# Four changes of order on TensorE in a fused decoder block: residual transposes, score pairs, probability transposes, first square sum

## The chip, the cores and the metric

The kernel runs on one core of a Trainium2 chip. The metric is the device time of one execution in microseconds (us); the times given are of three runs, and one more execution was recorded by the hardware profiler. Engines are called as the profile calls them: PE is TensorE (matmuls), PEld its weight loads, DVE is VectorE, ACT is ScalarE, POOL is GpSimd, SP is SyncE, which here issues the DMAs.

## What is computed

One decoder block on 256 tokens of width 1024, in float32: a hybrid mixer (a convolution branch and a dilated attention branch with 12 heads of 64, both gated), then a retrieval layer that picks 16 of 16384 single-neuron experts for each of 8 heads. Cut to what matters:

```python
xn = rmsnorm(x, norm1_g)
proj = xn @ w_in                                  # GLU input, q, k, v, gates
conv_out = conformer_conv(glu_in, ...)            # 31 taps, layernorm, silu, projection
q, k = rmsnorm(q, q_norm_g), rmsnorm(k, k_norm_g) # per head
s = q @ k.T * scale + bias[head, distance]        # per head, causal, dilated windows
p = exp(s - logsumexp(s)) ; o = p @ v             # times a weight per head group
merged = sigmoid(g_conv) * conv_out + sigmoid(g_attn) * (o @ attn_w_proj)
x = x + merged @ mix_w_out
hn = rmsnorm(x, norm2_g)
q = hn @ w_q ; s = q . sub_keys ; top 16 of 16 x 16 candidates ; gate = softmax
h = u_tab[e] . hn ; act = gelu(h) * gate ; y = x + sum(act * v_tab[e])
```

## The kernel before

**Tiles.** All weights come as tiles of 128 x 1024 float32 (512 KB), through a ring of four slots. Tiles 0 to 75 are the front: 0 to 7 GLU, 8 to 19 q and k, 20 to 25 v, 26 to 41 gates, 42 to 47 attention projection, 48 to 51 convolution projection, 52 to 59 mixer output, 60 to 75 the queries of the retrieval (`wq` 0 to 15, "query tiles"). Then 128 tiles of `u_tab` and 128 of `v_tab` follow in loops. Each tile is split into a high part (ACT, `split_hi`, L335) and a low part (POOL or DVE, `split_lo`, L354); the activations are split as well, so one tile is 8 blocks times 3 products (high by high, high by low, low by high): 24 matmuls at L1218, L1319 or, for the first tiles, L1242 and L1249. A tile's slot is loaded again when its low part is there, ACT and POOL work three tiles ahead of PE.

**Order.** `jobs_in_order()` (L81) writes out by hand, tile by tile, which results PE makes in the front; the tables `SCORES_AT`, `TURN_AT`, `ATTEND_AT` and others say after which tile small jobs stand. From this list come the number of PE's step that each consumer waits for, and the PSUM bank of each job (`BANK_OF`, L130): six banks in turn up to the first transposed probabilities, then seven, then eight, and from the first mixer tile on banks 4 to 7 only. `start(job)` lets PE wait until the bank's previous job has been read by ACT or DVE. For the third query tile and those behind it this is the query tile or square sum four jobs ahead, so `wq` 3 waits for DVE's scaled copy of `wq` 0 (L982).

**The places of the change.**
- `first_tiles()` (L1253): the first three GLU tiles are multiplied before the norm of x is known; behind them stands the sum of squares `ssq1` (L1265, `ones` by `sq`). ACT takes its root (L493), DVE its reciprocal (L764), and all of DVE's and ACT's later work on the norm, up to the high and low parts of the normed x that tile 8 needs, hangs on it. In DVE's queue the last addition of squares (L760) stands behind the low part of tile 3 (`lo_of(3)`).
- `scores(two)` (L1325): two score jobs at a time. Job s is for token half c = s // 6 and the pair of heads `PAIRS[s % 6]`, which are (0, 2), (1, 3), (4, 6), (5, 7), (8, 10), (9, 11). An even head lies in SBUF partitions 0 to 63 of its q and k block, an odd one in 64 to 127, and so in rows 0 to 63 or 64 to 127 of the array. For c = 0 a head's product has 128 columns, for c = 1 it has 256. The loop alternates between the two jobs: first head of one, first head of the other, second heads.
- On DVE `score(s)` (L818, L825) adds the bias and takes the maximum, on ACT `exp_of(s)` takes the exponentials (L507), both counting on semaphores in order.
- `turn(h)` (L1340) transposes a head's probabilities, three blocks of 128 x 128; `attend(bl)` (L1349) multiplies two heads' transposed probabilities with the values. The four slots of `pT` are used in turn, so the copy of head h's transposes waits for the product that read head h - 4.
- The residual transposes (L1440): 16 transposes of the new residual x into banks 0 to 3, where the retrieval's result is then accumulated. POOL fills `iota_nk` (L456) after them, on the semaphore `y_began`.
- `q_sums`, `k_sums`, `spread_k`: norms of q and k. `spread_k` (L1306) needs `rk_parts` from DVE (L900), which stands in DVE's queue between the taps of the depthwise convolution (L794, L798).

Of the kernel before, what the change touches and what calls it, by code (L numbers as in the profile page):

```python
# [15 lines left out]
P = 128  # L16
D = 1024
T = 256
KB = D // P
TC = T // P  # L20
# [43 lines left out]
QSS_AT, KSS_AT, KB_AT = 16, 20, 22  # L64
SCORES_AT = {24: (0, 1), 25: (2, 3), 26: (4, 5), 27: (6, 7), 28: (8, 9), 30: (10, 11)}
WEIGHTS_AT = 32
# [16 lines left out]
def jobs_in_order():  # L83

    order = []
    for n in range(T_ATT):
        if n < T_QK:
            order.append((("glu", n), n))
            if n == 2:
                order.append((("ssq1",), None))  # L90
        elif n < T_V:
            order.append((("qk", n - T_QK), n))
        elif n < T_GATE:
            order.append((("v", (n - T_V) // 2) if (n - T_V) % 2 else None, n))
        else:
            order.append((("gate", n - T_GATE), n))
        order += [(("bias", h), None) for h in BIAS_AT.get(n, ())]
        if n == QSS_AT:
            order.append((("qss",), None))
        if n == KSS_AT:  # L100
            order.append((("kss",), None))
        if KB_AT <= n < KB_AT + AB // 2:
            order.append((("kb", n - KB_AT), None))
        order += [(("score", i), None) for i in SCORES_AT.get(n, ())]
        if n == LNSUM_AT:
            order.append((("lnsum",), None))
        if n == LNVAR_AT:
            order.append((("lnvar",), None))
        order += [(("o", bl), None) for bl in ATTEND_AT.get(n, ())]
        order += [(("pT", h), None) for h in TURN_AT.get(n, ())]  # L110
    for b in range(KB):
# [54 lines left out]
def hybrid_block(nc, x_t, front, cols, rel_bias, onehot, sub_keys, u_tiles, v_tiles, out):  # L166
    bias_row = nc.dram_tensor("bias_row", (HEADS, BW), F32, kind="Internal").ap()
    toeplitz = nc.dram_tensor("toeplitz", (HEADS, P * BW), F32, kind="Internal").ap()
    with ExitStack() as ctx:
# [295 lines left out]
        def _(a):  # L465
# [34 lines left out]
            def exp_of(s):  # L500
                c, pair = divmod(s, len(PAIRS))
                w = P * (c + 1)
                a.wait_ge(score_max, s + 1)
                for h in PAIRS[pair]:
# [197 lines left out]
        def _(dve):  # L702
# [50 lines left out]
            for i in range(2):  # L753
# [3 lines left out]
                   .then_inc(pair_sums, 1)  # L757
            lo_of(3)
            dve.wait_ge(pair_sums, 2)
            dve.tensor_tensor(sq[:, 0:2, :], sq[:, 0:2, :], part_, ALU.add).then_inc(pair_sums, 1)  # L760
            dve.wait_ge(prm_in, 16)
            dve.tensor_tensor(gains[:, :], prm[:, C_QG:C_QG + 1], prm[:, C_KG:C_KG + 1], ALU.mult).then_inc(gains_ready, 1)
# [47 lines left out]
            def score(s):  # L810
# [12 lines left out]
                freed(dve, ("score", s))  # L823
                dve.wait_ge(biased, s + 1)
                dve.tensor_reduce(negm[:, c * HEADS + h0:c * HEADS + h0 + 3:2], p3[:, h0:h0 + 3:2, c * P:c * P + w],  # L825
# [39 lines left out]
            def attention_after(n):  # L865
                for b in ATTEND_AT.get(n, ()):
                    low_o(b)
                for h in TURN_AT.get(n, ()):
                    if freed_by_dve(("pT", h)):
                        copy_pT(dve, dve.tensor_copy, h)  # L870

            for n in range(T_ATT):
# [325 lines left out]
        def _(pe):  # L1198
# [54 lines left out]
            def first_tiles():  # L1253

                b0, b1, b2 = [start(("glu", n)) for n in range(3)]
                high_products(b0, 0)
                high_products(b1, 1)
                low_products(b0, 0)
                low_products(b1, 1)
                high_products(b2, 2)  # L1260
                low_products(b2, 2)
                b = start(("ssq1",))
                pe.wait_ge(pair_sums, 3)
                for k in range(2):
                    ins = pe.matmul(b[:, 0:T], ones[:, :], sq[:, k, :], start=k == 0, stop=k == 1)  # L1265
                step(ins)

            def two_tiles(jobs, tiles, parts_ready, vec_hi, vec_lo):
# [56 lines left out]
            def scores(two):  # L1325

                c = two[0] // len(PAIRS)
                w = P * (c + 1)
                banks = [start(("score", s)) for s in two]
                freed(pe, ("kb", two[0] % len(PAIRS) // 2))  # L1330
                for r in range(2):
                    for b, s in zip(banks, two):
                        h = PAIRS[s % len(PAIRS)][r]
                        rows = slice((h % 2) * HD, (h % 2 + 1) * HD)
# [27 lines left out]
            for n in range(T_ATT):  # L1362
# [38 lines left out]
                if n == min(TURN_AT):  # L1401
                    pe.wait_ge(tap, CB * TAPS)
                    freed(pe, ("v", AB // 2 - 1))
                for bl in ATTEND_AT.get(n, ()):
                    attend(bl)
                for h in TURN_AT.get(n, ()):
                    turn(h)
            for b_ in range(KB):
# [24 lines left out]
            for u in range(2, HALVES):  # L1433
                step(full(T_WQ + u, ("wq", u), xg_hi, xg_lo))
                if u == 2:

                    freed(pe, ("mix", KB - 1))
                    for c in range(TC):
                        for k in range(KB):
                            ins = pe.matmul(bank[2 * c + k // 4][:, (k % 4) * P:(k % 4 + 1) * P],  # L1440
                                            resid[:, k, c * P:(c + 1) * P], ident[:, :], is_transpose=True,
                                            start=k % 4 == 0, stop=False, skip_group_check=True)
                    ins.then_inc(y_began, 1)
            assert done[0] == FRONT_STEPS
            pe.wait_ge(sk_in, 16)
            for j in range(N_SC):
# [181 lines left out]
```

## Time and profile before

| | |
|---|---|
| median of 3 runs | 996.57 us (996.49 to 997.5) |
| the profiled execution | 997.07 us, span in the profile 995.2 us |
| PE busy | 989.8 us, 99% of the span |
| DVE, ACT, POOL busy | 774.9, 506.8, 465.3 us |
| granted clock of PE | 1.0 of full speed |
| front (tiles 0 to 75 and the scores of the keys) | to about 259.5 us |
| u tiles, v tiles | 259.5 to 626, 626 to 992 us |

An ended line of the timeline gives start, duration, engine, source line, operation and operands; rows of one kind that follow each other are merged ("x8"), and a matmul's duration holds its latency, so the pace of PE is read from starts, or from the chain of waits, whose rows run from one start of a group to about the next. A float32 matmul is two records, an fp32r matmul and a transpose one.

### The profile page before, as it was taken

Reading aid. Unit: us, or ns where it says so; the run is one execution under the profiler, and the core shown is the slowest. Engines: PE = TensorE matmul, PEld = TensorE weight load, DVE = VectorE, ACT = ScalarE, POOL = GpSimd, SP = SyncE. Lnnn points to the kernel's source line nnn. Section 1 sums busy time; section 2 is a strip of 40 time slices with the busy share of each in tenths; the row PEclk is TensorE's granted clock in tenths of the full one; section 3 lists DMA queues with packets and bytes.
Section 4 is the critical chain, followed back from the end, with each engine's and each line's share of the span. In section 5 each row is a group of like instructions: output and inputs, shape, how many; then the busy total and the mean of one; then the engine's idle time right before and its main releaser. Section 6 shows DMA issues by size and latency. Waiting matters only on the chain.

```text
span 995.2 us, 21854 instructions
## 1 busy us (share of the span) xinstructions
PE 989.8 (99%) x7822; PEld 917.0 (92%) x7822; DVE 774.9 (78%) x1304; ACT 506.8 (51%) x789; POOL 465.3 (47%) x198
## 2 busy tenths in 40 slices
PE   9999999999999999999999999999999999999998
PEld 9998999999999999999999999888888888888887
DVE  5999784868899996097777777988888876776764
ACT  6663877544555544544444444444444445554443
POOL 3664366656689999874444444100000004344442
PEclk9999999999999999999999999999999999999999
DMA  6684445654455565555555555555554555556562
GB/s 242 211 308 150 149 148 162 212 201 149 150 197 200 171 211 188 191 176 184 177 180 174 182 172 169 185 175 170 177 180 171 182 174 190 190 189 195 186 203 90
DMA packets 52619, 181.95 MB, mean 183 GB/s; under 512 B 5943, under 2 KB 9155, under 8 KB 52452
## 3 DMA queue, kind: packets, MB, share of 16 engines
q1 hardware_dynamic: 52292, 181.16, 54.4%
q8 instruction: 25, 0.41, 0.2%
q10 hardware_dynamic: 288, 0.27, 0.1%
q14 instruction: 14, 0.11, 0.0%
HBM read 180.33 MB, written 3.43 MB: 185 GB/s over the span
## 4 chain that ended last, share of the span: by engine, by line
PE 93%; DVE 5%; ACT 1%; issue 0%; POOL 0%; ACTq 0%; DVEq 0%; POOLq 0%
PE bank L1218 50%; PE bank L1527 35%; DVE bank L798 3%; PE bank L1476 3%; PE bank L1319 1%; PE bank L1233 1%; PE bank L1451 1%; DVE lo L354 1%; PE bank L1242 1%; PE bank L1553 1%; PE bank L1335 1%; ACT hi L335 0%; PE bank L1358 0%; PE bank L1346 0%; PE bank L1249 0%
## 5 line engine op out<-in xcount | busy, mean ns | idle before, releaser
L354 POOL TENSOR_TENSOR lo<-raw,hi 128x1024 fp32r<-128x1024 f32 x184 | 462.4, 2527 | 515.9 <-ACT hi L335 515.4
L335 ACT CAST hi<-raw 128x1024 fp32r<-128x1024 f32 x332 | 348.0, 1049 | 218.0 <-PE bank L1527 186.3
L1218 PE MATMUL bank<-norm_space,hi 128*128 128x256 f32 x2624 | 452.4, 278 | 0.2 <-POOL lo L354 0.2
L1218 PEld LDWEIGHTS bank<-norm_space,hi 128*128 128x128 f32 x2624 | 396.2, 188 | 1.8 <-issue 1.2
L1218 PE MATMUL bank<-norm_space,lo 128*128 128x256 f32 x1312 | 362.8, 277 | 0.0
L1527 PE MATMUL bank<-hi,norm_space 128*128 128x512 f32 x1008 | 273.8, 391 | 0.0
L1218 PEld LDWEIGHTS bank<-norm_space,lo 128*128 128x128 f32 x1312 | 246.4, 188 | 0.0
L1527 PEld LDWEIGHTS bank<-hi,norm_space 128*128 128x128 f32 x1008 | 188.0, 188 | 38.5
L354 DVE TENSOR_TENSOR lo<-raw,hi 128x1024 fp32r<-128x1024 f32 x148 | 189.2, 1279 | 27.4 <-ACT hi L335 27.3
L1527 PE MATMUL bank<-lo,norm_space 128*128 128x512 f32 x504 | 155.5, 390 | 0.0
L1145 DVE TENSOR_TENSOR norm_space<-act,norm_space 128x256 fp32r<-128x256 f32 x128 | 111.7, 876 | 48.8 <-ACT norm_space L665 48.8
L645 ACT ACTIVATE act<-bank 128x256 f32 (+1 forms) x128 | 49.2, 384 | 187.8 <-PE bank L1218 187.8
L1527 PEld LDWEIGHTS bank<-lo,norm_space 128*128 128x128 f32 x504 | 94.6, 188 | 19.7
L1218 PE MATMUL bank<-rounded_space,hi 128*128 128x256 f32 x496 | 87.0, 280 | 0.0
L1138 DVE SCALAR_TENSOR_TENSOR act<-bank,act 128x512 f32 (+1 forms) x64 | 41.4, 686 | 51.7 <-PE bank L1476 51.7
L1126 DVE TENSOR_TENSOR ohB<-eqB,parts 128x1024 f16<-128x1024 f16 x64 | 81.4, 1272 | 0.0
L1218 PEld LDWEIGHTS bank<-rounded_space,hi 128*128 128x128 f32 x496 | 75.4, 188 | 0.9 <-issue 0.6
L1218 PE MATMUL bank<-rounded_space,lo 128*128 128x256 f32 x248 | 69.1, 278 | 0.0
L665 ACT CAST norm_space<-act 128x256 fp32r (+1 forms) x128 | 51.4, 402 | 0.1
L1218 PEld LDWEIGHTS bank<-rounded_space,lo 128*128 128x128 f32 x248 | 47.0, 190 | 0.0
L798 DVE SCALAR_TENSOR_TENSOR bank<-u_pad,prm,bank 128x256 f32<-128x256 f32 x116 | 46.3, 481 | 0.0
L1122 DVE TENSOR_TENSOR ohA<-iota_nk,keys 128x1024 f16<-128x1024 f16 x64 | 46.1, 720 | 0.0
(183 smaller groups left out, 651.5 us busy)
## 6 DMA issues: line engine op xcount, KB each, us to landing
raw<-u_tiles SPq DMA_DIRECT2D x128, 512.0 KB, 3.3
raw<-v_tiles SPq DMA_DIRECT2D x128, 512.0 KB, 3.3
raw<-front SPq DMA_DIRECT2D x76, 512.0 KB, 3.8
toeplitz<-bias_row SPq DMA_DIRECT2D x6, 384.0 KB, 7.5
bias<-toeplitz SPq DMA_DIRECT2D x12, 128.0 KB, 3.5
resid<-x_t SPq DMA_DIRECT2D x2, 512.0 KB, 4.7
qk<-sub_keys SPq DMA_DIRECT2D x1, 1024.0 KB, 8.0
y<-act SPq DMA_DIRECT2D x3, 256.0 KB, 2.0
```

Source lines behind the costliest of these rows:

```text
L335: act_e.copy(hi[:, s, :], raw[:, s, :]).then_inc(hi_ready, 1)
L354: eng.tensor_tensor(lo[:, s, :], raw[:, s, :], hi[:, s, :].bitcast(F32), ALU.subtract)\
L645: a.activation(act[:, it * 4 + (base_i + j), :], bank[4 + j % 2][:, 0:T], ACT.Gelu).then_inc(gelu_done, 1)
L665: a.copy(act_hi[:, (base_i + j) % RING, :], act[:, it * 4 + (base_i + j), :]).then_inc(a_hi, 1)
L798: dve.scalar_tensor_tensor(out=acc[:, b, :] if w == TAPS - 1 else part_sum, in0=src, scalar=wt, in1=part_sum, op0=ALU.mult, op1=ALU.add).t ...
L1122: dve.tensor_tensor(ohA[:, g % 2], every_pair(iota_nk[:, :, :], NK), at(keys[:, 0, t], NK), ALU.is_equal).then_inc(spread, 1)
L1126: dve.tensor_tensor(ohB[:, g % 2].rearrange("p a i n b -> p (a i) n b"), eqB[:, :, :, :].unsqueeze(2).broadcast_to([P, TOK // PAIR, 2, HAL ...
L1138: dve.scalar_tensor_tensor(out=av, in0=gv, scalar=1.0 / GATE_SCALE, in1=av, op0=ALU.mult, op1=ALU.mult)\
L1145: dve.tensor_tensor(act_lo[:, s, :], act[:, it * 4 + (base_i + j), :], act_hi[:, s, :].bitcast(F32), ALU.subtract).then_inc(a_lo, 1)
L1218: ins = pe.matmul(dst, w_[:, s, u * P:(u + 1) * P], x_[:, k, :], start=first and i == 0 and p_ == 0, stop=last and i == n - 1 and p_ == 2)
L1476: ins = pe.matmul(bank[6 + g][:, q * HALF:(q + 1) * HALF], ohA[:, g, q // PAIR, :, q % PAIR], ohB[:, g, q // PAIR, i, :, q % PAIR], start= ...
L1527: ins = pe.matmul(bank[2 * c + half][:, :], a_[:, j, c * P:(c + 1) * P], v_[:, j, half * 512:(half + 1) * 512], start=False, stop=False, s ...
```

## The change

Four edits, and what follows from them in the counters:

1. The residual transposes go from behind `wq` 2 to behind `wq` 15, ahead of the key scores (L1451).
2. `SCORES_AT` pairs a job of the second token half with the job of the first half for the same heads: (6, 0), (7, 1) and so on, where it was (0, 1), (2, 3). `SCORE_PLACE` gives each job's place in the new order for the two semaphores that count.
3. Behind tiles 38 and 39 the transposes of the probabilities (`pT`) come ahead of the products with the values (`o`), on PE, in the bank order and on DVE. ACT's order stays.
4. `ssq1` comes behind the second tile, the third tile behind it; DVE's last addition of squares comes ahead of the low part of tile 3.

```diff
-SCORES_AT = {24: (0, 1), 25: (2, 3), 26: (4, 5), 27: (6, 7), 28: (8, 9), 30: (10, 11)}
+SCORES_AT = {24: (6, 0), 25: (7, 1), 26: (8, 2), 27: (9, 3), 28: (10, 4), 30: (11, 5)}
+SCORE_PLACE = {s: i for i, s in enumerate(s for n in sorted(SCORES_AT) for s in SCORES_AT[n])}
...
-            if n == 2:
+            if n == 1:
                 order.append((("ssq1",), None))
...
+        order += [(("pT", h), None) for h in TURN_AT.get(n, ())]
         order += [(("o", bl), None) for bl in ATTEND_AT.get(n, ())]
-        order += [(("pT", h), None) for h in TURN_AT.get(n, ())]
...
-                a.wait_ge(score_max, s + 1)
+                a.wait_ge(score_max, SCORE_PLACE[s] + 1)
...
-            lo_of(3)
             dve.wait_ge(pair_sums, 2)
             dve.tensor_tensor(sq[:, 0:2, :], sq[:, 0:2, :], part_, ALU.add).then_inc(pair_sums, 1)
+            lo_of(3)
...
-                c = two[0] // len(PAIRS)
-                w = P * (c + 1)
                 banks = [start(("score", s)) for s in two]
                 freed(pe, ("kb", two[0] % len(PAIRS) // 2))
                 for r in range(2):
                     for b, s in zip(banks, two):
-                        h = PAIRS[s % len(PAIRS)][r]
+                        c, pair = divmod(s, len(PAIRS))
+                        w = P * (c + 1)
+                        h = PAIRS[pair][r]
...
             for u in range(2, HALVES):
                 step(full(T_WQ + u, ("wq", u), xg_hi, xg_lo))
-                if u == 2:
-
-                    freed(pe, ("mix", KB - 1))
-                    for c in range(TC):
...
+            freed(pe, ("mix", KB - 1))
+            for c in range(TC):
+                for k in range(KB):
+                    ins = pe.matmul(bank[2 * c + k // 4][:, (k % 4) * P:(k % 4 + 1) * P],
+                                    resid[:, k, c * P:(c + 1) * P], ident[:, :], is_transpose=True,
+                                    start=k % 4 == 0, stop=False, skip_group_check=True)
+            ins.then_inc(y_began, 1)
```

On PE at its first products (L1242 and L1249 are high and low part of a tile, bank0 and bank1 the first two tiles), before:

```order
L1249 MATMUL bank1<-rounded_space,lo 128x256 x8
L1242 MATMUL bank2<-rounded_space,hi 128x256 x16
L1249 MATMUL bank2<-rounded_space,lo 128x256 x8
L1265 MATMUL bank3<-sq,ones 128x256 x2
L1218 MATMUL bank4<-rounded_space,hi 128x256 x2
```

and after (lines are numbered one or two higher):

```order
L1250 MATMUL bank1<-rounded_space,lo 128x256 x8
L1264 MATMUL bank2<-sq,ones 128x256 x2
L1243 MATMUL bank3<-rounded_space,hi 128x256 x16
L1250 MATMUL bank3<-rounded_space,lo 128x256 x8
L1219 MATMUL bank4<-rounded_space,hi 128x256 x2
```

The square sum now stands ahead of the third tile's 24 products.

On PE the first call of `scores`, behind tile 24, before (bank1 is score job 0, heads 0 and 2; bank2 is job 1, heads 1 and 3):

```order
L1335 MATMUL bank1<-qk 128x128
L1335 MATMUL bank2<-qk 128x128
L1335 MATMUL bank1<-qk 128x128
L1335 MATMUL bank2<-qk 128x128
```

and after (bank1 is job 6, heads 0 and 2 for the second token half; bank2 is job 0, heads 0 and 2 for the first):

```order
L1337 MATMUL bank1<-qk 128x256
L1337 MATMUL bank2<-qk 128x128
L1337 MATMUL bank1<-qk 128x256
L1337 MATMUL bank2<-qk 128x128
```

Each of the six calls now has one wide and one narrow job, and all four of its matmuls are of heads of the same parity.

On PE at the end of the front, after the change, behind the last query tile:

```order
L1441 MATMUL bank0<-ident,resid 128x128 x4
L1441 MATMUL bank1<-ident,resid 128x128 x4
L1441 MATMUL bank2<-ident,resid 128x128 x4
L1441 MATMUL bank3<-ident,resid 128x128 x4
L1451 MATMUL bank7<-qk,prob 128x128 x4
L1451 MATMUL bank4<-qk,prob 128x128 x4
```

The sixteen transposes stood between `wq` 2 and `wq` 3, whose products now follow each other directly.

## Rows read from the trace of the kernel before

**Rows 1.** The page: busy time, share of the span and instructions of each engine.

```profile
PE 989.8 (99%) x7822; PEld 917.0 (92%) x7822; DVE 774.9 (78%) x1304; ACT 506.8 (51%) x789; POOL 465.3 (47%) x198
```

**Rows 2.** Waits of PE: who is waited for, us in total, times, longest.

```profile
PE bank L1306 <- DVE rk_parts L900: 0.8, 1, 0.8
PE bank L1218 <- POOL lo L354: 0.2, 1, 0.2
```

**Rows 3.** Chain that ended last: start us, us, what. Two score calls, key scores.

```profile
91.27 0.65 PE bank L1335 x8
...
102.10 1.06 PE bank L1335 x8
...
252.52 7.14 PE bank L1451 x64
```

**Rows 4.** Timeline: start us, us, engine, line. Weight loads beside the square sum's matmuls.

```profile
210.24 0.59 PE L1431 MATMUL bank<-sq,ones 128*128 128x256 f32 x2
210.46 0.40 PEld L1432 LDWEIGHTS bank<-sq,ones 128*128 128x128 f32 x2
210.67 0.59 PE L1432 MATMUL bank<-sq,ones 128*128 128x256 f32 x2
```

**Rows 5.** Chain that ended last, long stretches of tiles at two paces.

```profile
153.06 57.34 PE bank L1218 x504
...
215.77 36.75 PE bank L1218 x312
```

**Rows 6.** Timeline of PE and DVE around the residual transposes.

```profile
212.46 1.75 DVE L989 RECIPROCAL rs<-rs 128x256 f32<-128x256 f32 x1 [3.36 <-ACT rs L633]
214.25 0.42 DVE L982 TENSOR_TENSOR prob<-bank,rs 128x256 f32<-128x256 f32 x1
```

```profile
213.86 1.91 PE L1440 MATMUL bank<-ident,resid 128*128 128x128 f32 x16
215.52 0.48 PE L1218 MATMUL bank<-rounded_space,hi 128*128 128x256 f32 x2
```

**Rows 7.** Timeline of DVE, from the squares to the first tap.

```profile
13.20 0.69 DVE L756 TENSOR_TENSOR bank<-sq,bank 128x512 f32<-128x512 f32 x1
...
19.48 1.75 DVE L764 RECIPROCAL rs<-rs 128x256 f32<-128x256 f32 x1 [2.96 <-ACT rs L493]
...
28.16 1.22 DVE L354 TENSOR_TENSOR lo<-raw,hi 128x1024 fp32r<-128x1024 f32 x1
...
35.34 0.43 DVE L777 TENSOR_TENSOR bank<-bank,rs 128x256 f32<-128x256 f32 x1 [0.24 <-PE bank L1218]
...
38.67 2.78 DVE L354 TENSOR_TENSOR lo<-raw,hi 128x1024 fp32r<-128x1024 f32 x1 [0.57 <-ACT hi L335]
41.38 1.88 DVE L794 TENSOR_SCALAR bank<-u_pad,prm 128x256 f32<-128x256 f32 x4
```

**Rows 8.** Timeline of ACT: high parts of tile 4, root, tiles 5 and 6.

```profile
16.29 1.05 ACT L335 CAST hi<-raw 128x1024 fp32r<-128x1024 f32 x1 [2.22 <-DMA raw<-front]
19.06 0.38 ACT L493 ACTIVATE rs<-bank 128x256 f32<-128x256 f32 x1 [1.72 <-PE bank L1265]
...
20.76 2.00 ACT L335 CAST hi<-raw 128x1024 fp32r<-128x1024 f32 x2
```

**Rows 9.** Timeline of POOL: low parts of tiles 5 and 6, then 8 to 10.

```profile
21.89 4.77 POOL L354 TENSOR_TENSOR lo<-raw,hi 128x1024 fp32r<-128x1024 f32 x2 [2.09 <-ACT hi L335]
32.92 7.44 POOL L354 TENSOR_TENSOR lo<-raw,hi 128x1024 fp32r<-128x1024 f32 x3 [6.27 <-ACT hi L335]
```

**Rows 10.** Timeline of PE: two tile starts, at 24.44 and 35.47.

```profile
24.22 0.28 PE L1218 MATMUL bank<-rounded_space,lo 128*128 128x256 f32 x1
24.44 0.47 PE L1218 MATMUL bank<-rounded_space,hi 128*128 128x256 f32 x2
...
35.02 0.28 PE L1218 MATMUL bank<-rounded_space,lo 128*128 128x256 f32 x1
35.47 0.47 PE L1218 MATMUL bank<-norm_space,hi 128*128 128x256 f32 x2 [0.17 <-POOL lo L354]
```

More of the change, by code:

```diff
@@ L823, in score @@
                 freed(dve, ("score", s))
-                dve.wait_ge(biased, s + 1)
+                dve.wait_ge(biased, SCORE_PLACE[s] + 1)
                 dve.tensor_reduce(negm[:, c * HEADS + h0:c * HEADS + h0 + 3:2], p3[:, h0:h0 + 3:2, c * P:c * P + w],
@@ L865, in attention_after @@
             def attention_after(n):
-                for b in ATTEND_AT.get(n, ()):
-                    low_o(b)
                 for h in TURN_AT.get(n, ()):
@@ L870, in attention_after @@
                         copy_pT(dve, dve.tensor_copy, h)
+                for b in ATTEND_AT.get(n, ()):
+                    low_o(b)
             for n in range(T_ATT):
@@ L1253, in first_tiles @@
             def first_tiles():
-                b0, b1, b2 = [start(("glu", n)) for n in range(3)]
+                b0, b1 = [start(("glu", n)) for n in range(2)]
                 high_products(b0, 0)
@@ L1259, in first_tiles @@
                 low_products(b1, 1)
-                high_products(b2, 2)
-                low_products(b2, 2)
                 b = start(("ssq1",))
@@ L1266, in first_tiles @@
                 step(ins)
+                b2 = start(("glu", 2))
+                high_products(b2, 2)
+                low_products(b2, 2)
             def two_tiles(jobs, tiles, parts_ready, vec_hi, vec_lo):
@@ L1403, in _ @@
                     freed(pe, ("v", AB // 2 - 1))
+                for h in TURN_AT.get(n, ()):
+                    turn(h)
                 for bl in ATTEND_AT.get(n, ()):
                     attend(bl)
-                for h in TURN_AT.get(n, ()):
-                    turn(h)
             for b_ in range(KB):
@@ L1434, in _ @@
                 step(full(T_WQ + u, ("wq", u), xg_hi, xg_lo))
-                if u == 2:
-                    freed(pe, ("mix", KB - 1))
-                    for c in range(TC):
[L1439 to L1443, printed above, removed]
-            assert done[0] == FRONT_STEPS
+            assert done[0] == FRONT_STEPS
+            freed(pe, ("mix", KB - 1))
[5 more added lines that the diff above has]
+            ins.then_inc(y_began, 1)
             pe.wait_ge(sk_in, 16)
```

## The prediction

> **What bounds the kernel now.** The page first: PE is busy 99% of the span, and every other engine has room [rows 1]. Then PE's own waits: apart from its start they come to 1.0 us, 0.8 of it for DVE's `rk_parts` and 0.2 for a low part from POOL [rows 2]. So the time is the sum of what PE issues, and there is little waiting to remove: an edit pays only by PE's pace, by these waits, or by gaps too small for the list of waits. The order of reading: waits of PE, the chain of waits (it gives the pace of each stretch), then the timeline of PE at each place of the change with that of the engine it hangs on. Durations are from one profiled execution of 997.07 us (span 995.2, 1.9 around it). Its distance to the median, 0.5 us, is as large as some terms below; I work out the difference and put it on the median, 996.57 us.
>
> **Pace of PE.** The chain shows long stretches of the same product line at two paces: 504 products (21 tiles) in 57.34 us are 113.8 ns each, but the 312 products (13 query tiles) right behind the residual transposes take 36.75 us, 117.8 ns each, without a wait among them [rows 5]. The stretch at the fast pace reaches to the square sum `ssq2`, and `wq` 2 behind that has the same pace. The slow pace costs 24 x 4.4 = 0.11 us a tile.
>
> **Part 1, residual transposes behind the query tiles.** The 16 transposes take 215.52 - 213.86 = 1.66 us [rows 6] in the old place and the same in the new, so they cancel. Two things don't.
> The gain: if `wq` 3 to 15 keep the pace that `wq` 2 has, 13 tiles x 0.11 = 1.4 us.
> The cost: the transposes cover a wait. `wq` 3 uses the bank of `wq` 0, which is free once DVE's scaled copy L982 has read it. DVE begins this at 214.25 and ends it at 214.67, behind a reciprocal of 1.75 us, which itself follows ACT's root [rows 6]. PE is through with `wq` 2 at 213.86, so without the transposes it stands until about 214.8 (the copy's end and a hand-over of some 0.15 us): 0.95 us, and about 0.1 us for starting again, together 1.0 us. Nothing shortens DVE's side. Net: -0.4 us if the pace stays fast, +1.0 us if the restart leaves it slow. The trace has few restarts in the middle of a stream: at 24.44 and at 35.47 [rows 10]; the tiles behind the first go at about 118 ns, those behind the second at 113. I take fast, by the row nearest in kind (a wait of more than 0.2 us). POOL's `iota_nk` moves 1 us later, and its next low part is not due for several us; no cost. The key scores behind the transposes wait for nothing now; no gain.
>
> **Part 2, score pairs.** A call for the first half takes 0.65 us and one for the second half 1.06 us [rows 3]. They are 8 records each. Full-height float32 records cost (210.67 - 210.24) / 2 = 0.215 us at 256 columns [rows 4] and 7.14 / 64 = 0.112 us at 128 columns [rows 3]; eight in a row would be 1.72 and 0.89 us. The calls are shorter, because even heads sit in rows 0 to 63 of the array, odd heads in 64 to 127, and the halves work beside each other: each half has four records, 4 x 0.112 = 0.45 and 4 x 0.215 = 0.86, and 0.20 us of filling and emptying comes on top in both cases. That model gives both rows. After the change the two jobs of a call are of the same pair of heads, so all eight records use the same 64 rows and nothing runs beside them: 4 x 0.215 + 4 x 0.112 + 0.20 = 1.51 us. Six calls: 9.05 us against 3 x 0.65 + 3 x 1.06 = 5.13 us, **+3.9 us**. Bound from below: the narrow job still hides beside the wide one, 1.06 us a call, 6.4 us, +1.2 us. Bound from above: no load of weights hides any more (a rival below). I take +3.9, since it is made of rows that agree. The added time stands on PE's path, as PE waits for nobody there; DVE and ACT get a wide and a narrow job each time, the same work in all, and lag PE by banks that were free 2 us and more before their turn.
>
> **Part 3, transposes ahead of the products with values.** The same instructions, in another order, in two places. What changes is which hand-overs between full-width and half-width matmuls occur (about 0.1 us each, as many as before) and the pace of the gate tile behind, which now follows products and not transposes: 2 x 0.11 us at stake. Copies of heads 4 to 7 wait for the products as before and have a gate tile of 2.8 us to finish. I take 0, with 0.2 us to both sides.
>
> **Part 4, the first square sum sooner.** The sum is ready to be taken sooner: DVE's second pair sum ends at 13.89 [rows 7], the last addition (0.7 us) then at about 14.6, and PE reaches the new place at 15.3, one tile of 2.7 us before 18.0. PE's own work is the same. ACT stands ready for the root only at 17.34, behind the high part of tile 4, which its DMA holds until 16.29; so the root comes at 17.4 and not at 19.06, 1.7 us sooner [rows 8]. With it:
> - The high parts of tiles 5 and 6 begin 1.7 us sooner than 20.76 [rows 8], and POOL's low part of tile 5 ends near 22.5, not at 24.3 [rows 9]. PE's start of tile 5 at 24.44 (0.22 us behind the previous record, where 0.113 is normal) [rows 10] loses its gap: 0.1 us, 0.1 for the restart, 0.2 if the two tiles behind it get the fast pace: 0.4 us.
> - Tile 8 starts at 35.47, 0.45 us behind the previous record, on the low part of POOL that began at 32.92 [rows 9, 10]: 0.3 us go.
> - DVE does its norms sooner, and then waits for tile 7 at 35.34 as it does now (0.24) [rows 7]. Behind that the low part of tile 11 took 2.78 us, over twice the 1.22 of the one at 28.16, while POOL was busy to 40.36 beside it, and it waited 0.57 us for ACT. With POOL and ACT ahead by more than a microsecond, the first tap comes 0.5 (tile 7 alone) to 1.9 us before 41.38. From there to `rk_parts` DVE works without a pause, so the 0.8 us that PE waits for it [rows 2] go, if the taps are ahead by what PE itself gains and 0.8 more: about 1.5 us. I take that; the rows of the low part carry most of it.
> Together -1.5 us (-0.5 to -1.6).
>
> **Sum.** +1.0 - 1.4 + 3.9 + 0 - 1.5 = **+2.0 us**: 996.57 + 2.0 = 998.6 us, 0.2% slower. What a measurement of this kernel can tell from no change is about 0.2%, 2 us: the forecast sits on that edge.
>
> **Rivals.**
> - *The query tiles stay slow.* The restart at `wq` 3 falls into the 117.8 ns pace, as the one at 24.44 did. Then the wait is paid and nothing gained: +3.4 us, 1000.0 us. For it: what stood ahead of the slow stretch was a break in the stream, as here. Against: 35.47 was one too.
> - *The start brings nothing.* DVE's taps come only 0.5 us sooner, because tile 7, ACT's bias rows or the DMAs hold them: -0.5 in place of -1.5, +3.0 us, 999.6 us. Against: ACT's and POOL's rows all hang on the root.
> - *The score jobs still overlap* (the other side: not slower). If a call costs 1.06 us, as the wide pair did, part 2 is +1.2 and the sum -0.7 us: 995.9 us. The side changes at a call of (5.13 + 1.9) / 6 = 1.17 us. Against it speaks that full-height records in one place are each paid in full [rows 3, 4] and that only different row halves ever overlapped.
> - *Loads of weights come into the open.* A call's first record is followed 0.1 us late, and in the same 64 rows that could happen to each: 7 x 0.1 x 6 = 4.2 us more, 1002.8 us. Against it: at the square sum the next weights load from 210.46 on, while the matmul that starts then still uses all rows [rows 4]. The Trainium skill, "TensorE: Matmul & The Clock Gate", Part 3, says that a weight load overlaps running matmuls only where its row group is another one; by that rule this rival would be the forecast, and the row at 210.46 does not agree with it.
> - *The change does not do what it says* is not open: the order of the built program shows all four moves.
>
> **How the numbers follow.** Forecast 0.45; query tiles slow 0.22; start brings nothing 0.15; overlap 0.08; loads in the open 0.04; 0.06 for paces of the other front tiles falling differently (some 17 tiles beside the 13 are slow now, 0.11 us each; all changes of neighbours can turn them, to both sides). The forecast's own range is 997.4 to 999.4. The 8 in 10 take in the first two rivals: 997.0 to 1000.5. Slower by over 0.2% (over 998.6): half of the forecast, nearly all of three rivals: 0.60. Faster by over 0.2% (under 994.6) needs the overlap and every gain: 0.04. Within: 0.36.
>
> **What would show it.** Scores: each call of the new kernel 1.5 us from its first record to the next tile. Query tiles: a gap of about 0.95 us on PE ahead of `wq` 3, ended by DVE's L982 copy, then 13 tiles of 2.72 us (2.83 if the rival holds). Start: ACT's root at 17.4, no gap ahead of tiles 5 and 8, no wait for `rk_parts`. Wrong would be: calls near 1.1 us; no gap at `wq` 3; DVE's first tap still near 41 us.

## The result, and the profile after

The changed kernel takes 1007.68 us (median of 4 runs, 1007.07 to 1008.01) against 996.53 us for the kernel before beside it: 1.0107 times the time, with an interval of 1.0095 to 1.0118. Forecast were 998.6 us and a range of 997.0 to 1000.5; the side was right, the size was not, and the median lies 7.2 us above the range. The profiled execution takes 1007.57 us with a span of 1005.8 us, 10.6 us longer than the span before, so the profile shows nearly the whole difference.

The page (busy time and share of the span) and the waits of PE (who is waited for, us in total, times, longest), kernel after:

```profile
PE 1000.5 (99%) x7822; PEld 927.7 (92%) x7822; DVE 766.0 (76%) x1304; ACT 507.0 (50%) x789; POOL 464.3 (46%) x198
```

```profile
PE bank L1219 <- DVE prob L983: 0.7, 1, 0.7
PE bank L1308 <- DVE rk_parts L901: 0.2, 1, 0.2
```

PE has the same 7822 instructions as in [rows 1] and is busy 10.7 us longer. The list of waits is hardly longer (apart from the 1.2 us at the start, which both kernels have): one new wait of 0.7 us, while that for `rk_parts` went from 0.8 [rows 2] to 0.2. Waits can't be the answer; PE does the same work more slowly. The chain that ended last tells where (start us, us, what), first of after:

```profile
89.15 1.50 PE bank L1337 x8
...
115.75 8.38 PE bank L1219 x72
124.13 0.86 PE bank L1395 x4
124.99 10.91 PE bank L1219 x96
...
154.02 59.22 PE bank L1219 x501
...
217.90 37.02 PE bank L1219 x312
254.91 1.75 PE bank L1441 x16
256.66 7.15 PE bank L1451 x64
263.81 169.67 PE bank L1219 x1440
433.48 0.44 PE bank L1491 x4
```

and of before, one piece of the gate tiles, and the piece of the same 60 tiles of `u_tab`:

```profile
113.97 8.68 PE bank L1218 x72
```

```profile
259.66 163.29 PE bank L1218 x1440
422.95 0.44 PE bank L1491 x4
```

The 1440 products behind the key scores, in which nothing was changed, take 169.67 and not 163.29 us: 117.8 against 113.4 ns each. The 504 products from tile 41 (the last gate tile behind the products with values) to tile 61 ("x501": three records are counted elsewhere) go at 59.22 / 501 = 118.2 ns, where [rows 5] has 113.8. Put together, in us, with the starts of the chain (the first product of each from the timeline of PE, 9.74 and 8.96):

| stretch | before | after | difference |
|---|---|---|---|
| start to the first product | 9.74 | 8.96 | -0.8 |
| to the first `spread_k` (83.29, 81.17) | 73.55 | 72.21 | -1.3 |
| scores and gate tiles, to 153.06 and 154.02 | 69.77 | 72.85 | +3.1 |
| 504 products, `ssq2`, query tiles, without transposes | 97.71 | 100.89 | +3.2 |
| transposes and key scores | 8.89 | 8.90 | 0.0 |
| 1440 products of u tiles | 163.29 | 169.67 | +6.4 |
| the rest | 572.25 | 572.32 | +0.1 |
| span | 995.2 | 1005.8 | +10.6 |

The first line is no effect of the change: in the fourteen recorded executions of this document, one of each kernel, PE's first product comes anywhere from 8.85 us (`p1_only`) to 9.74 us (before), and `p3_only`, which is changed only far behind it, has 9.72.

**How a pace begins.** These rows are the timeline of PE (start us, us, engine, line, what) where the u tiles begin, before:

```profile
259.49 0.47 PE L1218 MATMUL bank<-norm_space,hi 128*128 128x256 f32 x2
259.80 0.28 PE L1218 MATMUL bank<-norm_space,lo 128*128 128x256 f32 x1
259.92 0.40 PE L1218 MATMUL bank<-norm_space,hi 128*128 128x256 f32 x2
260.16 0.28 PE L1218 MATMUL bank<-norm_space,lo 128*128 128x256 f32 x1
260.27 0.39 PE L1218 MATMUL bank<-norm_space,hi 128*128 128x256 f32 x2
260.50 0.28 PE L1218 MATMUL bank<-norm_space,lo 128*128 128x256 f32 x1
260.61 0.39 PE L1218 MATMUL bank<-norm_space,hi 128*128 128x256 f32 x2
```

and after:

```profile
263.64 0.47 PE L1219 MATMUL bank<-norm_space,hi 128*128 128x256 f32 x2
263.95 0.28 PE L1219 MATMUL bank<-norm_space,lo 128*128 128x256 f32 x1
264.06 0.40 PE L1219 MATMUL bank<-norm_space,hi 128*128 128x256 f32 x2
264.30 0.28 PE L1219 MATMUL bank<-norm_space,lo 128*128 128x256 f32 x1
264.42 0.40 PE L1219 MATMUL bank<-norm_space,hi 128*128 128x256 f32 x2
264.65 0.28 PE L1219 MATMUL bank<-norm_space,lo 128*128 128x256 f32 x1
```

Three products are one period, from "hi" x2 to "hi" x2. Before: 259.92, 260.27, 260.61: 0.35, then 0.34 us, and 0.34 from there on, 163.29 us long. After: 264.06, 264.42, then 0.353 us for all 480 periods. From record to record before has 103, 194, 117, 117, 123, 118, 113, 114, 113 ns, after 104, 193, 117, 118, 118, 118, 117, 118, 118 ns. The first records are alike; then one stream finds the short step and the other does not, and neither changes until something else interrupts it. That holds throughout: in the fourteen recorded executions no uninterrupted run of 20 or more of these products changes its pace behind its sixth record. The granted clock is 1.0 in both stretches.

The weight loads on PEld tell which part of a product grows. In both kernels a load starts 3.3 ns (mean) behind the start of the product before it. From the start of a load to the start of its own product pass 110.0 ns in the u stream of before and 114.4 ns in that of after, and the same two numbers separate fast from slow in the streams of 504 and in the query tiles. So the whole 4.4 ns lie between the start of a load and the start of its product; what happens there the traces don't show.

### The profile page after: what moved, and what is told of

Read it like the earlier page. It is cut to its first block, busy times and chain, and to the rows that moved or that the text cites. A ratio compares the mean times of both kernels' runs of the same rounds, so it can differ in the third digit from the quotient of the medians.

```text
span 1005.8 us, 21854 instructions
## 1 busy us (share of the span) xinstructions
PE 1000.5 (99%) x7822; PEld 927.7 (92%) x7822; DVE 766.0 (76%) x1304; ACT 507.0 (50%) x789; POOL 464.3 (46%) x198
## 4 chain that ended last, share of the span: by engine, by line
PE 91%; DVE 5%; DMA 1%; ACT 1%; issue 1%; POOL 0%; SPq 0%; DVEq 0%; ACTq 0%
PE bank L1219 49%; PE bank L1527 34%; DVE bank L799 3%; PE bank L1476 3%; DMA raw<-front 1%; PE bank L1337 1%; PE bank L1321 1%; PE bank L1451 1%; ACT hi L336 1%; PE bank L1553 1%; DVE lo L355 0%; PE bank L1360 0%; PE bank L1348 0%; POOL lo L355 0%; DVE norm_space L720 0%
## 5 line engine op out<-in xcount | busy, mean ns | idle before, releaser
L1219 PE MATMUL bank<-norm_space,hi 128*128 128x256 f32 x2624 | 458.8, 279 | 0.0
```

What stands on the lines that cost most here:

```text
L1219: ins = pe.matmul(dst, w_[:, s, u * P:(u + 1) * P], x_[:, k, :], start=first and i == 0 and p_ == 0, stop=last and i == n - 1 and p_ == 2)
```

## The experiments

Two questions were put: which edit costs what, and whether the pace of a stream is decided where it begins. "Fast" and "slow" below are the paces of 113.4 and 117.8 ns a product in the recorded execution, for the three long streams (a stream is a run of these products with nothing else on PE between them): 504 (tiles 41 to 61), query tiles (`wq` 3 to 15, or 2 to 15), u (1440). Where the executions of one kernel fall apart into two groups, both are given; their medians are 5.5 to 7.0 us apart.

| kernel | time, us (executions) | 504 | query | u |
|---|---|---|---|---|
| before | 996.21 to 997.95 (72 beside the experiments) | fast | slow | fast |
| after | 1007.07 to 1008.01 (4) | slow | slow | slow |
| `p1_only` | 996.12 to 997.4 (6), 1002.91 to 1004.83 (4) | fast | fast | fast |
| `p2_only` | 1000.0 (6) | fast | slow | fast |
| `p3_only` | 996.83 (1), 998.47 to 999.26 (9) | slow | slow | fast |
| `p4_only` | 995.7 (10) | fast | slow | fast |
| `after_undo1` | 1000.92 (5) | slow | slow | fast |
| `after_undo3` | 998.45 to 999.6 (6), 1004.7 to 1004.93 (4) | fast | slow | fast |
| `p2_crossed` | 998.11 (10) | fast | slow | fast |
| `p4_ssq2` | 994.4 to 994.58 (4), 1000.87 to 1002.95 (6) | fast | fast | fast |
| `after_u1` | 1001.19 (4) | slow | fast | fast |
| `after_u2` | 1001.07 (1), 1007.49 to 1010.88 (4) | slow | fast | fast |
| `undo1_a1` | 998.87 (10) | fast | slow | fast |
| `ssq2_f16` | 994.98 (10) | fast | fast | fast |

Of the kernels with two groups it was each time an execution of the faster group that was recorded, so that their slower group has slow u tiles is concluded from the distance alone: the stream of 1440 products gives 6.4 us, the query tiles at the other pace about 1 us more or less. The pace of single streams in executions that were not recorded is not shown. In the recorded execution of `undo1_a1` the fast stream is 480 products, tiles 42 to 61; tile 41 stands ahead of the added matmul.

### Each edit alone

**Edit 1 alone**, `p1_only`: the kernel before, with the transposes behind the query loop.

```diff
-                if u == 2:
-                    (16 transposes)
+            (16 transposes, behind the loop over u)
```

> The kernel before with the residual transposes moved behind the query tiles, nothing else. Theory A (restart): a stream of fp32r products runs at 113.4 or 117.8 ns each, and which one is set in the first products behind a break, by the instructions right around it. The break ahead of query tile 3 (now a wait of about 0.95 us) and the one ahead of the u tiles (transposes, key scores, first u tile) are here the same as in the changed kernel, so both streams run slow: 13 query tiles 36.8 us as before, 1440 u products 169.7 us instead of 163.3. Sum +1.0 + 6.4 = +7.4 us, 1004.0 us. Theory B (the whole program's shift in time, or other engines' traffic, sets the pace): the u tiles keep 113.4 ns, since all engines do there what they did; +1.0 us at most, 997.5 us.

The wait ahead of `wq` 3 came as forecast: 988 ns from record to record. In the recorded execution the query tiles behind it were fast, and the u tiles as well, where theory A expected both slow every time. But the executions fall into two groups: the lower one (median 997.1) is 0.4 us above the kernel before beside it (996.7), the upper one 7.3. The edit that was booked with -0.4 can cost 7.

**Edit 2 alone**, `p2_only`:

```diff
-SCORES_AT = {24: (0, 1), 25: (2, 3), ...
+SCORES_AT = {24: (6, 0), 25: (7, 1), ...
```

> The kernel before with the score pairs alone in the new order. Six calls of 1.50 us instead of 0.65 and 1.06: +3.9 us. Theory A: the gate tiles between the calls run as in the changed kernel (two slow, the rest fast, where nine were slow: -0.7 us), and the 21 tiles behind the attention products and the u tiles, whose breaks are those of before, stay at 113.4 ns: 999.7 us. Theory B: the later part of the program is shifted by 3 us as in the changed kernel, so the long streams may run slow as there: up to 1008 us.

1000.0 us, +3.3 (ratio 1.0029, interval 1.0017 to 1.0042). Each of the six calls is 1.50 us long, one group of executions. The streams behind the calls start 3.0 us later than in the kernel before and take 57.34, 36.75 and 163.29 us, exactly as there: a shift in time alone does not change their pace (theory B).

**Edit 3 alone**, `p3_only`:

```diff
+        order += [(("pT", h), None) for h in TURN_AT.get(n, ())]
         order += [(("o", bl), None) for bl in ATTEND_AT.get(n, ())]
-        order += [(("pT", h), None) for h in TURN_AT.get(n, ())]
... (the same swap in the instructions of PE and DVE)
```

> The kernel before with the transposes of probabilities ahead of the products with values, nothing else. Theory A: the last products with values now follow a gate tile at the fast pace, as in the changed kernel, and the 21 tiles behind run at 117.8 ns (59.5 us instead of 57.3, +2.2); two gate tiles become fast (-0.2); the u tiles stay fast. 998.6 us. Theory B: a reorder of 3 us of work cannot matter: 996.5 us, or all long streams slow.

998.91 us, +2.2 (1.0010 to 1.0029). The chain of this kernel (start us, us, what) says where, against 57.34 in [rows 5]:

```profile
152.94 59.56 PE bank L1218 x504
```

With the transposes ahead, the gate tiles 39 and 40 follow the products with the values and are fast (0.34 us for three products, 0.35 before); a round of transposes, products with values and gate tile takes 5.69 instead of 5.75 us. Behind the last products with values the stream of 504 then starts slow, +2.22 us. One execution of the ten took 996.83 us, as if that start had gone the other way; it was not recorded.

**Edit 4 alone**, `p4_only`:

```diff
-            if n == 2:
+            if n == 1:
                 order.append((("ssq1",), None))
... (PE's third tile behind the square sum, DVE's last addition of squares ahead of `lo_of(3)`)
```

> The kernel before with the first square sum a tile sooner, nothing else. In the changed kernel PE reached the first matmul behind rk_parts 2.1 us sooner than before. Theory A: that gain is kept whole, since all later breaks are those of before: 994.5 us, with the 21 tiles and the u tiles at 113.4 ns. Theory B: the shift of 2 us can change the pace of the long streams: 994.5 us or some us more.

995.7 us, -1.0 (0.998 to 1.000), where 994.5 us was expected. PE still waits 0.7 us for `rk_parts` here; in the kernel after it was 0.2.

The four alone are +7.3 (upper group), +3.3, +2.2 and -1.0, together 11.8; measured for all are 11.1. With the lower group of `p1_only`, +0.4, the sum is 4.9: the difference is the u stream's pace.

### One edit undone

**`after_undo1`** is the kernel after with the transposes back behind `wq` 2; **`after_undo3`** has the order of before for `pT` and `o`.

> The changed kernel with the residual transposes back between query tiles 2 and 3. The move alone gave two kinds of executions, about 996.8 and 1004 us, and in its recorded one (996.12 us) the query tiles and the u tiles both ran at 113.4 ns. Theory A2 (inherited pace): with the transposes behind them, the query tiles hand their pace on through transposes and key scores to the 1440 u products, while the key scores alone, behind slow query tiles, lead to fast u tiles, as in the kernel before. Then here the query tiles run slow (behind transposes), the u tiles fast, in every execution: 1007.7 - 1.0 - 6.4 = 1000.3 us. Theory B (time shift or traffic sets the pace): some executions keep slow u tiles, 1006.7 us.

> The changed kernel with products with values ahead of the transposes again. Theory A2: the last products with values follow a gate tile, whose pace (as behind transposes in the kernel before) is slow, and the 21 tiles behind run at 113.4 ns: -2.2 us in every execution. The query tiles behind the wait can come out at either pace and hand it on, so executions fall into two groups: 1007.7 - 2.2 + 0.2 = 1005.6 us and 7.8 us less, 997.8 us. Theory B: one group near 1007 us.

`after_undo1` gives 1000.92 us: 6.8 us of the 11.1 go with edit 1. The u tiles are fast again, and by the times (1000.72 to 1001.77) in all five executions. From its chain:

```profile
263.55 163.29 PE bank L1219 x1440
```

`after_undo3` gives 998.45 to 999.6 in six executions and 1004.7 to 1004.93 in four: the 504 products are fast again, and with them the start of the u tiles, in which nothing was edited, is no longer slow each time. The wait ahead of `wq` 3 is in it. From its chain:

```profile
215.98 37.02 PE bank L1219 x312
...
261.89 163.29 PE bank L1219 x1440
```

Slow query tiles, then transposes and key scores, then fast u tiles: so a stream does not hand its pace on through what stands between (theory A2). The lower group was forecast by it at 997.8 us with both streams fast, and came at 998.45 to 999.6.

### Does the score call lose its overlap because of the rows of the array?

**`p2_crossed`** keeps a wide and a narrow job in each call but takes heads of opposite parity:

```diff
-SCORES_AT = {24: (0, 1), 25: (2, 3), 26: (4, 5), ...
+SCORES_AT = {24: (6, 1), 25: (7, 0), 26: (8, 3), ...
```

> The kernel before with wide and narrow score jobs in turn, but of heads of opposite parity: (6, 1), (7, 0), (8, 3), (9, 2), (10, 5), (11, 4). Row halves as the cause of part 2's price: the narrow job works in the other 64 rows beside the wide one, each call takes 4 x 0.215 + 0.20 = 1.06 us, 6.4 us in all, +1.2 us instead of +3.9; with the gate tiles as in the run of part 2 alone 997.3 us. If instead alternating two widths costs in itself: calls of 1.5 us and 1000 us as there.

998.11 us. The first call's weight loads on PEld and matmuls on PE, first of the same parity (kernel after):

```profile
89.08 1.38 PEld L1337 LDWEIGHTS bank<-qk 64*128 64x128 f32 x8
```

```profile
89.08 1.57 PE L1337 MATMUL bank<-qk 64*128 64x256 f32 x8
```

and crossed:

```profile
90.43 0.73 PEld L1336 LDWEIGHTS bank<-qk 64*128 64x128 f32 x8
```

```profile
90.43 1.13 PE L1336 MATMUL bank<-qk 64*128 64x256 f32 x8
```

The chain has 1.50 us for the same-parity call and 1.06 for the crossed one, as wide as the wide call alone in [rows 3]. So the narrow job hides beside the wide one when it uses the other 64 rows, and is paid in full when it uses the same. With that, edit 2 costs 6 x (1.50 - 1.06) = 2.6 us more than crossed pairs; 1000.0 - 998.11 is 1.9 (2.3 when each is taken against the median of the kernel before beside it, 996.7 and 997.11). The rest is pace again: the 72 and 96 products behind the last call take 8.68 and 11.31 us with crossed pairs and 8.38 and 10.91 us in `p2_only`, 0.7 us. That is also most of what 998.11 lies above the 997.3 expected. Pairing wide with narrow is itself a loss, six calls of 1.06 us where 5.13 us stood in all, +1.2 (measured +1.0). The rival with loads in the open fell too: in a same-parity call only the first record is 0.1 us late (0.320 us to the next), and those behind it start 0.216, 0.109, 0.112, 0.218, 0.216 and 0.109 us apart, the rates of records with hidden loads. The Trainium skill ("TensorE: Matmul & The Clock Gate", Part 3) says in its list of what overlaps that a load overlaps running matmuls only in another row group; the 1.50 us do not agree with that sentence: all eight use the same 64 rows, and seven of the eight loads cost nothing.

### Is a stream's pace decided at its start?

If it is, some work at the start of a slow stream alone, adding time, must give back the 6.4 or 2.2 us. **`after_u1`** and **`after_u2`** add one or two float32 matmuls of `ident` with `ident` (two records each, 0.22 us, into columns that nobody reads) ahead of the first u tile of the kernel after; **`undo1_a1`** adds one to `after_undo1` ahead of attention projection tile 42, that is, behind the first 24 of the 504 products.

```diff
+            for _ in range(1):
+                pe.matmul(bank[4][:, T:T + P], ident[:, :], ident[:, :], start=True, stop=True)
             for j in range(RING):
                 u_tile(0, 0, j)
```

> The changed kernel with one more float32 matmul (identity by identity, 128 columns, two records, 0.22 us) between the key scores and the first u tile, into a free half of bank 4; its result is not used. Theory C: the pace of the 1440 u products is set by how their first records fall in time on the records and weight loads ahead (nanoseconds), so an added 0.22 us can turn it: the u products come out at 113.4 ns, 163.3 us instead of 169.7, and the kernel with more work takes 1007.7 + 0.2 - 6.4 = 1001.5 us. Theory B (later traffic of POOL, DVE or the DMAs, or the place of the code, slows them): 1007.9 us.

> As the kernel with one more matmul, with two (four records, 0.45 us). Theory C: fast or slow as it falls, the same in nearly all executions, 1001.7 or 1008.1 us; if one of the two kernels is fast, C holds. Theory B: 1008.1 us, both slow.

> The changed kernel with the residual transposes back in their place (1000.9 us, 21 tiles behind the last products with values slow in every execution), and one more float32 matmul of identity by identity between these products and the first tile of the attention projection. Theory C: these 504 products can come out at 113.4 ns, 57.3 us instead of 59.5: 1000.9 + 0.2 - 2.2 = 998.9 us; slow would be 1001.1. Theory B: 1001.1 us.

`after_u1`: 1001.19 us (1000.76 to 1001.9), 6.5 us less than the kernel after, with one matmul more. Its chain:

```profile
256.31 7.15 PE bank L1451 x64
263.46 0.29 PE bank L1482 x2
263.74 163.22 PE bank L1219 x1440
```

163.22 for 169.67 us, 6.45 less. (The query tiles were fast as well in this execution, -1.1 with the wait it brings ahead of `wq` 15; the added matmul and a score part that begins 0.7 us later take most of that back.) `undo1_a1`: 998.87 us where `after_undo1` has 1000.92, in all ten executions, and in its chain tiles 42 to 61 are fast (the first row is tile 41):

```profile
154.28 3.02 PE bank L1219 x24
157.30 0.22 PE bank L1413 x2
157.52 54.42 PE bank L1219 x480
```

54.42 / 480 is 113.4 ns. So both excesses lie in the pace, and a new start can change it. How firmly the added matmul is the reason differs. For tiles 42 to 61 it is firm: by the times slow in all five executions of `after_undo1` and fast in all ten of `undo1_a1`. For the u tiles it is four executions (slow) against four (fast), of a stream that came out either way from execution to execution in `p1_only` and `after_undo3`. If each execution of `after_u1` had the six chances in ten of these two, u tiles at 113.4 ns all four times would come by luck in 0.6 x 0.6 x 0.6 x 0.6 = 13% of cases, an estimate from their counts. `after_u2` shows that the amount of added work is no rule: one execution was at 1001.07, the four others at 1007.49 to 1010.88, though here the restart followed the same kind of matmul as in `after_u1`. That missed its expectation of one pace in nearly all executions. Theory C, that the nanoseconds of the first records decide, agrees with these runs and is not shown by them: nothing here sets that timing.

### A version that beats both

**`p4_ssq2`** is the kernel before with edit 4, and with the transposes ahead of `wq` 2, right behind `ssq2`, where they cover DVE's work for `wq` 0 as well as before.

```diff
+            (16 transposes, ahead of wq 2)
             for u in range(2, HALVES):
                 step(full(T_WQ + u, ("wq", u), xg_hi, xg_lo))
-                if u == 2:
-                    (16 transposes)
```

> The kernel before with the first square sum sooner (part 4, 995.7 us alone), and the residual transposes between the second square sum and query tile 2, where they still cover the wait for the copy of query tile 0 and share a break with the square sum. One break less: -0.1 us. The pace of query tiles 2 to 15 is set by one restart behind transposes, whose neighbours are not those of any run so far. Theory A2: fast, 994.1 us, then the u tiles (key scores alone ahead) may be either, since only slow query tiles were seen ahead of key scores alone; slow, 995.5 us as now with fast u tiles. Theory B says nothing of the pace; 995.6 us.

Four executions at 994.4 to 994.58, six at 1000.87 to 1002.95. The query tiles were fast, 35.38 us for 312 products, and then a new gap came: 0.31 us from record to record ahead of `wq` 15, where 0.113 is normal. The timeline of DVE of `p1_only`, where the query tiles are fast too, has the low part of that tile:

```profile
243.63 3.09 DVE L354 TENSOR_TENSOR lo<-raw,hi 128x1024 fp32r<-128x1024 f32 x1
```

It ends at 246.72, and PE goes on with `wq` 15 at 246.87. **`ssq2_f16`** adds sixteen fp16 matmuls of 64 columns ahead of the u tiles. Blocks of this kind stand between the later u tiles in all the kernels. The stream behind the first block of sixteen is fast in the other recorded executions and those behind blocks of 32 in all; but behind the second block of sixteen it is slow in every one (48 products in 5.73 us, 5.54 where fast), and in `ssq2_f16` it is slow behind both of these later ones. So this kind of block is no rule for a fast start.

```diff
+            half = ident[:, :].bitcast(F16)
+            for _ in range(16):
+                pe.matmul(bank[4][:, T:T + 64], half[:, 0:P], half[:, 0:64], start=True, stop=True)
             for j in range(RING):
                 u_tile(0, 0, j)
```

> The kernel with part 4 and the residual transposes between second square sum and query tile 2, which had executions at 994.4 and at 1001 us (fast query tiles, u tiles at either pace). Here 16 fp16 matmuls of 64 columns (0.5 us, result not used) stand ahead of the first u tile: behind the first group of 16 such matmuls all recorded traces have a fast stream. Theory C: one group near 994.4 + 0.5 = 994.9 us. If the pace were inherited from the query tiles whatever stands between, or random, two groups remain, 994.9 and 1001.3 us.

994.98 us (994.76 to 995.36, ten executions, one group, where `p4_ssq2` has six of ten in the upper one), 0.998 times the kernel before (0.9971 to 0.9990): a gain of 0.2%, small but outside the interval. It is 1.3% under the changed kernel. Its chain:

```profile
209.45 1.75 PE bank L1437 x16
211.20 35.38 PE bank L1218 x312
246.59 2.98 PE bank L1218 x24
249.58 7.14 PE bank L1450 x64
256.72 0.47 PE bank L1482 x16
257.19 163.31 PE bank L1218 x1440
```

## Why the prediction missed

**Scores, forecast +3.9: right, with a part given back.** The calls are 1.50 us, forecast 1.51, so the model with 64 rows held, and `p2_crossed` shows it. Of the 3.9 us 0.8 came back, nearly all since gate tiles between and behind the calls started fast: 8.38 for 8.68 us at 115.75, and 0.4 us in the 96 products at 124.99. The sum held no term for them.

**The wait ahead of `wq` 3, forecast +1.0: right.** The row of PE in the kernel after (in brackets idle time and who ended it):

```profile
217.90 0.50 PE L1219 MATMUL bank<-rounded_space,hi 128*128 128x256 f32 x2 [0.71 <-DVE prob L983]
```

990 ns from the record before it, where 113 is normal, behind DVE's copy from 217.42 on.

**The fast query tiles, forecast -1.4: wrong in this kernel.** 37.02 us for 312 products is the slow pace, the rival with 0.22. The choice was made by two restarts, one of each kind. `p1_only`, `after_u1` and `after_u2` have them fast behind the same wait, the kernel after and `after_undo3` slow: neither was the rule. In `after`, `after_u1` and `after_u2` even all of PE's instructions up to there are the same. And where they are fast, 0.3 us are lost again ahead of `wq` 15, so that the term could be -1.1 at best.

**Edit 3, forecast 0 with 0.2 to both sides: the step that failed, first part.** The prediction counted the gate tile behind each place at 0.11 us. What stands behind the last of them is 21 tiles without an interruption, and they lost 2.2 us together. The prediction had that stream in front of it, in [rows 5], as a fast one, and did not ask what made it fast.

**Transposes ahead of the key scores, no term at all: the step that failed, and most of the miss.** "The key scores behind the transposes wait for nothing now; no gain" looked at waits, and the sum at the place of the edit. The first u tile starts 9 us after it, behind 64 unchanged matmuls, and decides over 1440 products: 6.4 us. That it hangs on edit 1 is shown by `after_undo1` (u fast in all executions, 6.8 us less), and that it is pace alone by the two chains. Edit 1 makes the slow start possible and not certain: alone, and with edits 2 and 4 (`after_undo3`), it gave slow u tiles, by the times, in four executions of ten. All four of the kernel after are slow; whether edit 3 makes that certain or four executions are too few to see a fast one stays open. The unit of account was a tile, 0.11 us; it has to be the stream up to the next interruption. With 0.22 for slow query tiles and 0.06 for other tiles' paces, bounded by "some 17 tiles beside the 13", the range could not reach 1007. (The 4.4 ns take 113.4 for the fast pace, which the prediction's rows don't show; from their 113.8, which holds the first records too, it would be 4.0.)

**The start, forecast -1.5: right, a little too large.** -1.3 up to `spread_k` in the profile, -1.0 for the edit alone. That -1.3 is the upper end: counted from PE's first product, `spread_k` comes at 73.5 to 73.6 us in the five recorded kernels without edit 4 and at 72.2 to 73.0 in the nine with it, and the wait for `rk_parts`, forecast to go, is still 0.2 us in the kernel after and up to 0.9 (`after_u1`) in others. ACT's root, PE's first product taken as zero, comes 7.66 us in and not 9.32, 1.7 sooner:

```profile
16.62 0.38 ACT L494 ACTIVATE rs<-bank 128x256 f32<-128x256 f32 x1
```

The gaps ahead of tiles 5 and 8 are gone. The low part of tile 11 was as slow as before, 2.78 us behind 0.56 us of waiting for ACT, so the reason given for 1.5 rather than 0.5 (less beside it on POOL) did not come; DVE reached the taps sooner all the same, at 39.25, 1.35 us by the same count.

```profile
36.55 2.78 DVE L355 TENSOR_TENSOR lo<-raw,hi 128x1024 fp32r<-128x1024 f32 x1 [0.56 <-ACT hi L336]
39.25 1.88 DVE L795 TENSOR_SCALAR bank<-u_pad,prm 128x256 f32<-128x256 f32 x4
```

**The sum, again, with what was measured:** +1.0 (wait), 0 (query tiles), +3.1 (scores, gate tiles), +2.2 (504), -1.3 (start), +6.4 (u) = +11.4, with the earlier first product of this execution, 0.8, 10.6.

## What to carry to other kernels

Where PE is busy 99% of the time and one kind of product runs at two paces, the price of a reordering is not in the moved work but in the streams that restart behind it: list each interruption, the number of products to the next one, and the pace it has now, and let the range hold each fast stream turning slow (here 1440 x 4.4 ns). An unexplained fast pace is something that an edit can lose, even one whose own instructions cost nothing and stand several microseconds ahead. A single execution, or four, can show one pace of a stream that has two. When executions of one kernel fall into two groups, compare the groups, and look for a stream whose length times the difference of the paces is their distance.

## What the runs showed of the hardware

- A stream of fp32r products of 256 columns, each with its own load of weights, runs at 113.4 or 117.8 ns a product at the same granted clock of 1.0. It takes one of them within the first six records behind an interruption (another kind of instruction, or a wait) and kept it for as long as 1440 products. The difference lies between the start of a weight load and the start of its product: 110.0 ns where a product takes 113.4, 114.4 ns where it takes 117.8; the load follows the start of the product before by 3.3 ns in both.
- Behind the same interruption in the same kernel it can be either, from execution to execution (concluded from the times of the two groups). All four kernels with executions in two groups have a wait on PE in the query tiles; so have the kernel after, `after_u1` and `ssq2_f16`, which show one group, and one execution of `p3_only` stands 1.6 us off the nine others without such a wait. The kernels that have the u tiles behind 64 key scores and no such wait in the query tiles (before, `p2_only`, `p3_only`, `p4_only`, `after_undo1`, `p2_crossed`, `undo1_a1`) had no execution in an upper group.
- What in the array or its loads makes the two paces was not found, nor why the kernel after has slow u tiles each time while `p1_only` has them in four executions of ten. Where the operands lie in SBUF and where the code lies were not varied on their own.
- Two 64-row score jobs overlap when they use different halves of the rows, even with 256 columns beside 128: 1.06 us for what takes 1.50 us in one half.
